# The product of swished z with the returned outputs of mixers A and B: on GpSimd instead of VectorE

## What is computed

```python
merged = None
for i, y_i in enumerate((ya, yb, yc)):
    z = cols(COL_Z + i * BRANCH_WIDTH, BRANCH_WIDTH)
    g = cols(COL_G + i * D_MODEL, D_MODEL)
    u = jax.nn.sigmoid(g) * ((y_i * jax.nn.silu(z)) @ w_br[i])
    merged = u if merged is None else merged + u
out = merged @ w_out
return x + gate[:, None, :] * out
```

## Time and profile before

| | |
|---|---|
| median of 3 runs | 2335.7 us (2334.45 to 2336.24) |
| profiled execution, first to last instruction | 2334.2 us |
| TensorE busy | 2289.5 us |
| VectorE busy | 1669.9 us |
| ScalarE busy | 1123.4 us |
| GpSimd busy | 58.5 us |
| mean granted TensorE clock | 0.999 |

### The profile page before, as it was taken

How to read it: one execution, slowest core, us unless ns; L and a number is a source line. 1 busy time by engine, 2 the same in 40 slices (tenths; PEclk the granted TensorE clock), 3 DMA queues, 4 the chain that set the end, 5 groups by cost and what they waited for, 6 DMA issues and landing times.

```text
span 2334.2 us, 42068 instructions
## 1 busy us (share of the span) xinstructions
PE 2289.5 (98%) x15370; PEld 2135.9 (92%) x15370; DVE 1669.9 (72%) x4593; ACT 1123.4 (48%) x3077; POOL 58.5 (3%) x103
## 2 busy tenths in 40 slices
PE   7999999999999999999999999999999999999999
PEld 5888889999998999999888899899999989999998
DVE  7877677777765766676578867777877667676772
ACT  5666565444444443344356765754444353343440
POOL 0010110000000000000001002100000000000000
PEclk9999999999999999999999999999999999999999
DMA  7221321111113243221521121121110223333223
GB/s 283 95 76 56 122 62 60 58 57 60 56 64 103 74 125 118 93 90 64 173 82 35 35 82 44 58 83 60 56 59 33 82 99 99 102 113 97 88 89 119
DMA packets 74556, 198.72 MB, mean 85 GB/s; under 512 B 10864, under 2 KB 31984, under 8 KB 71408
## 3 DMA queue, kind: packets, MB, share of 16 engines
q1 hardware_dynamic: 59232, 170.29, 21.7%
q10 hardware_dynamic: 15120, 25.74, 3.1%
HBM read 175.02 MB, written 18.87 MB: 83 GB/s over the span
## 4 chain that ended last, share of the span: by engine, by line
PE 81%; DVE 8%; ACT 4%; issue 3%; DMA 3%; SPq 0%; DVEq 0%; ACTq 0%
PE ps_proj L1046 51%; PE ps_score L1092 8%; PE ps_pt L1092 7%; PE ps_pt L1241 2%; PE ps_score L1225 2%; PE ps_pv L1277 2%; PE ps_score L1209 1%; PE ps_pv L1258 1%; PE ps_tr L1292 1%; DMA y_part<-parked 1%; PE ps_tr L1293 1%; PE ps_pv L1271 1%; DVE top L2120 1%; DMA first_ada<-in_w_first 1%; DMA s_raw<-in_w_gate 1%
## 5 line engine op out<-in xcount | busy, mean ns | idle before, releaser
L1046 PE MATMUL ps_proj<-w_hi,act_hi 128*128 128x384 f32 x1824 | 633.7, 347 | 2.2 <-ACT act_hi L1502 1.3
L1046 PE MATMUL ps_proj<-w_hi,act_lo 128*128 128x384 f32 x1824 | 612.7, 336 | 0.0
L1046 PE MATMUL ps_proj<-w_lo,act_hi 128*128 128x384 f32 x1824 | 612.4, 336 | 0.0
L1046 PEld LDWEIGHTS ps_proj<-w_hi,act_hi 128*128 128x128 f32 x1824 | 343.1, 188 | 7.3 <-ACT act_hi L1502 4.8
L1046 PEld LDWEIGHTS ps_proj<-w_lo,act_hi 128*128 128x128 f32 x1824 | 343.8, 188 | 0.0
L1046 PEld LDWEIGHTS ps_proj<-w_hi,act_lo 128*128 128x128 f32 x1824 | 342.9, 188 | 0.0
L2049 DVE TENSOR_REDUCE ssq<-square 128x2 f32<-128x256 f32 (+1 forms) x228 | 95.6, 419 | 207.0 <-ACT square L1600 206.4
L1600 ACT ACTIVATE square<-ps_proj 128x256 f32<-128x256 f32 x228 | 88.1, 387 | 263.8 <-PE ps_proj L1046 263.4
L2426 DVE TENSOR_TENSOR w_lo<-w_raw,w_hi 128x1536 fp32r<-128x1536 f32 (+3 forms) x105 | 169.2, 1612 | 22.3 <-ACT w_hi L1426 21.5
L1426 ACT ACTIVATE w_hi<-w_raw 128x1536 fp32r<-128x1536 f32 (+2 forms) x104 | 144.3, 1388 | 42.5 <-DMA w_raw<-in_w 19.7
L2338 DVE TENSOR_TENSOR s_lo<-s_raw,s_hi 128x512 fp32r<-128x512 f32 x224 | 150.9, 686 | 1.7
(11 more groups left out here) (263 smaller groups left out, 5089.8 us busy)
## 6 DMA issues: line engine op xcount, KB each, us to landing
w_raw<-in_w SPq DMA_DIRECT2D x80, 768.0 KB, 5.7
s_raw<-in_w_gate SPq DMA_DIRECT2D x96, 256.0 KB, 3.2
w_ada<-in_w_mod SPq DMA_DIRECT2D x11, 1536.0 KB, 6.7
w_raw<-in_w SPq DMA_DIRECT2D x24, 512.0 KB, 3.8
wb_raw<-in_w_branch SPq DMA_DIRECT2D x24, 512.0 KB, 3.6
first_ada<-in_w_first SPq DMA_DIRECT2D x8, 1024.0 KB, 12.7
w<-in_w_gate SPq DMA_DIRECT2D x32, 256.0 KB, 3.8
parked<-y_t ACTq DMA_DIRECT2D x4, 1536.0 KB, 5.1
```

Of the source, the lines that this page charges most:

```text
L1046: op = pe.matmul(out, sta[s](k), mov[m](k), start=(k == 0 and n == 0), stop=(k == chunks - 1 and n == 2))
```

## The change

`swish_y` moves from VectorE's program to GpSimd's: the same waits, the same operands, the same semaphore raised. On GpSimd it is called at the same units, ahead of the biases of a unit. Nothing else differs.

```diff
--- before.py
+++ after.py
@@ -1032,8 +1032,16 @@
                             op = pool.tensor_tensor(out.rearrange("p (r k c) -> p r k c", r=4, k=4), win, mp, ALU.add)
                     op.then_inc(*bias_ready.inc((l, h, part)))
 
+            def swish_y(g, block_):
+
+                pool.wait_ge(*y_part_in.at((g, block_)))
+                pool.wait_ge(*swished.at((g, block_)))
+                pool.tensor_tensor(z_sig[block_][:], z_sig[block_][:], y_part[:], ALU.mult).then_inc(*yz_part.inc((g, block_)))
+
             pool.wait_ge(later_in, 16 * 4)
             for n, u in enumerate(UNITS):
+                for g, m in SWISHED_IN.get(n, ()):
+                    swish_y(g, m)
                 if u[0] == "q" and u[5] == 5 and (u[2] == "B" or u[2:4] == ("A", 3)) and u[2:4] != ("B", 3):
                     biases(u[1], (u[3] + 1) % HEADS)
 
@@ -2298,12 +2306,6 @@
                 value = ps_score[:, 0:HALF] if block_ == (0, 0) else sig_of[block_][:]
                 dve.tensor_tensor(z_sig[block_][:], value, z_sig[block_][:], ALU.mult).then_inc(*swished.inc((g, block_)))
 
-            def swish_y(g, block_):
-
-                dve.wait_ge(*y_part_in.at((g, block_)))
-                dve.wait_ge(*swished.at((g, block_)))
-                dve.tensor_tensor(z_sig[block_][:], z_sig[block_][:], y_part[:], ALU.mult).then_inc(*yz_part.inc((g, block_)))
-
             def combine(g, c):
 
                 before = group_before(g)
@@ -2490,8 +2492,6 @@
                             out_low(l, k)
                 if swishes and u2[4] == 4:
                     swish(u2)
-                for g, m in SWISHED_IN.get(n, ()):
-                    swish_y(g, m)
                 for a in TOPPED.get(n, ()):
                     if not first_tops:
                         tops(a)
```

## The result

Against the kernel before on the same chips (20 runs of each), the changed kernel takes 2340.2 us (2336.97 to 2344.7) where the kernel before takes 2336.2: a ratio of 1.002, 95% interval 1.0014 to 1.0026. It is slower by 4.0 us, with 3.3 to 6.1 inside the interval. Five of all the runs reported here took between 2806 and 7890 us, one of these 20 of the kernel before among them (4097.93 us), and are left out of every median. The forecast was 1.4 us faster, its range ended at 2340.0. The time lies just outside the range and on the other side of no change.

A forecast was written before the change was run, and what follows sets the result against it. TensorE, busy 98% of the span, was taken to bound the kernel, so only its waits counted. Gap two's −8.8 and gap one's +7.4 gave −1.4 us, 2335.7 to 2334.3 us, range 2329.8 to 2340.0.

The forecast's parts named there:

- gap two: TensorE's idle before unit T3 in each swished group, from VectorE waiting for y_part; closes, 1.10 us each, −8.8 in all.
- gap one: TensorE's idle before unit T2 in each swished group, ended by W21's load; grows 0.93 us each, +7.4 in all.
- The GpSimd product: The 128x384 float32 multiplication moved to GpSimd, 32 times, taken as 1.13 us each against VectorE's 0.56.
- The turns: GpSimd and VectorE each wait for the other's whole instruction, then finish their own usual time less 0.14 us.
- W21's landing: W21's load, issued behind the second y_part load, is issued and lands 0.93 us later, and T2 starts 0.93 later.
- The other blocks: Blocks two to four on GpSimd: third and fourth y_part loads go some 2 and 1 us earlier, off TensorE's path.
- Rival 2: Fourth block's GpSimd product holds up s_lo of W21, TensorE 0.45 us late per group, +3.6, 2337.9 us; chance 0.13.
- The store's path: First product's store to yz_kept, ahead of ScalarE's sigmoid and s_hi of T2, lands 0.9 us later, hidden by 1.7.
- Rivals 1, 3 and 4: GpSimd quicker, 2330.5, 0.20; GpSimd waiting until VectorE has no two-input work, 2347.7, 0.05; gap two staying, 2343.1, 0.04.
- Around the span: The 1.5 us between the profiled span and the median run time, taken as unchanged.

The follow-up runs named there:

- first_on_vector: Changed kernel with the first block's product back on VectorE, the other three on GpSimd; 2331.6 us, ratio 0.9981 to the kernel before.
- w21_first_gpsimd: Changed kernel with W21's load issued on SyncE ahead of the second block's y_part load; 2331.8 us, ratio 0.9983 to the kernel before.
- changed_look3: Changed kernel with no edit, a further profile; 2344.2 us, span 2342.1.
- both_ends_gpsimd: Changed kernel with W21's load ahead of the second y_part load and ScalarE's s_hi of T2 one unit earlier; 2330.4 us, ratio 0.9979.
- high_early_gpsimd: Changed kernel with only ScalarE's s_hi of T2 one unit earlier, SyncE's order as it was; 2339.3 us, ratio 1.0016 to the kernel before.
- late_load: Kernel before, all products on VectorE, with two idle loads put ahead of W21's load on SyncE; 2350.4 us, ratio 1.0062.
- changed_again: Changed kernel with no edit, run and profiled once more; 2339.3 us, ratio 1.0016 to the kernel before, span 2336.5.
- first_only_gpsimd: Changed kernel with only the first block's product on GpSimd, the other three back on VectorE; 2345.8 us, ratio 1.0039 to the kernel before.
- changed_look2: Changed kernel with no edit, a further profile; 2344.4 us, span 2342.3.
- w21_first_vector: Kernel before, all products on VectorE, with W21's load ahead of the second y_part load on SyncE; 2334.5 us, ratio 0.9993.
- third_later_vector: Kernel before with the third product one unit later on VectorE and its store one unit later on ScalarE; 2334.9 us, ratio 0.9998.
- both_ends_split: both_ends_gpsimd with the first block's product on VectorE and the other three on GpSimd; 2332.4 us, ratio 0.9987 to the kernel before.

## Why the prediction was wrong

**Which way it goes.** Right: TensorE's 16 waits are 8, gap two closes in all eight groups, gap one grows, and it grows through W21. first_on_vector and w21_first_gpsimd each cut one link of that chain, and each turns the loss into a gain.

**The GpSimd product.** Forecast 1.13 us alone; 1.01 to 1.02 measured, 0.12 less. The estimate of 0.84 for 384 columns, worked out from 4497 ns for 2048 (the Trainium skill, GPSIMD Engine Reference, "Elementwise — side-by-side cycle accounting"), is 0.17 too short; the measurement decides.

**The turns.** Right in kind. The first block's product takes 1.33 beside VectorE and 1.01 when VectorE stands still, and VectorE's two s_lo take 1.92 for 1.29. It ends at 814.30; from the start of the swish product that is 2.03 after, 1.21 before: 0.82 later, where 0.93 was forecast.

**Gap one.** Forecast +7.4. The first profile says +7.2, and 14.41 − 5.86 = +8.6 on the mean of four profiles. The product's 0.82 alone would make 6.6; what is above it is W21's landing, which takes 4.47 us on the mean of the eight groups before (4.2 to 4.8), and 4.55, 4.63, 4.68 and 4.97 in the four profiles after (4.1 to 6.2): 0.24 more in each group, 1.9 in all. The step moved W21's landing along with its issue and let it take as long as before. Why it takes longer on the mean, no run isolates.

**Gap two.** Forecast −8.8, measured −7.6 where nothing comes between: 11.57 less 10.62 in each of eight groups. The gap does go, but the term took every unit behind T2 at 2.08, and T4 and the b units still start a little late: the starts of W21, T4 and the b units (827.59, 829.74, 831.92) are 2.15 and 2.18 apart, 0.17 more than twice 2.08. The reading of before was a little high as well: by the prediction's own rule (T2 to b less 10.51) the eight groups are 1.02 to 1.13, 8.5 in all, where it had them at up to 1.17 and took 1.10. On the mean of four profiles it is −7.3, since four of their 32 groups take 0.2 to 0.5 more, by waits at T3, W21 or T4.

**The other blocks.** The third y_part load was forecast earlier by 2 us, as it was (issued at 818.36), but it landed 5.1 us later, not 3. So the third product began at 823.48, beside the s_lo of T3 that closes gap two, which took 0.93 for 0.68. It was hidden. Rival 2 (a meeting at the W21 unit) came in one of 32 groups of the changed kernel (0.35 us, in changed_look3), and in several of first_on_vector and both_ends_gpsimd, where the loads are earlier. Rivals 1, 3 and 4 didn't come. The store's path was hidden, as forecast; high_early_gpsimd bears that out.

**Around the span, and at its end.** Taken as 1.5 and unchanged; it is 1.80 (1.74 to 1.88) in the kernels without GpSimd products in all four blocks and 2.03 in the changed one: +0.24. Inside the span, VectorE's last operation starts 0.74 us after the start of the last matmul in the changed kernel and 0.39 before: +0.4. The sum has neither, and what they are, I don't know.

**The step that failed** is one that isn't there. The sum priced a pause of TensorE as its own length and put the clock behind it at nothing. Gap one went from 1.07 us at most to between 1.13 and 3.29, and behind some of the long ones TensorE ran for 3.4 us at 1.2 GHz, at 1.55 us each. late_load shows it with GpSimd idle, and neither kernel that splits the pause has one behind it. Over four profiles there are 8 spells, 2 to an execution: +3.1 us, against 1.2 missed at gap one and 1.5 at gap two.

These two misses alone turn the sign: +8.6 − 7.3 is +1.3, where −1.4 was forecast. That W21's landing would take as long as before, and that every unit behind T2 would take 2.08, are the two steps that had the direction wrong; the spells are the largest single miss and carry the time out of the range. The whole account on the mean of the four profiles is +8.6 − 7.3 + 3.1 + 0.4 (behind the last matmul) + 0.2 (ahead of and between the groups) = +5.0 on the span, and 5.2 with the 0.2 around it. Two of the four executions are among the slowest of this kernel, so this is more than the +4.0 by the medians. The mean clock of the 29 runs is 0.9982, that of the 96 of the kernel before 0.9993; at 3.4 us of half clock to a spell I estimate from it 1.5 spells more to an execution, +2.3 us, and +4.4 in all. The range missed the time for the same reasons: its upper end was put together from port meetings that hold up the W21 unit, of which one came in 32 groups. That it missed by only 0.2 us is luck: the meetings it was made of are not what made the kernel slow.

**What stays open.** Whether a given pause brings a spell isn't settled. The pauses with a spell behind them were 1.97 to 3.42 us long, and others of 2.00 to 2.30 (in changed_again, changed_look3, first_only_gpsimd and late_load) had none, so the length alone doesn't tell. The spell at 345 us, behind pauses of 1.02 us and less, says the same. Nor is it explained why some executions reach the first swished group 1.5 to 3.6 us late, changed_look2 and first_only_gpsimd among them: most of it is lost in the first 24 us of the program, far ahead of the moved work. In the three latest (first_only_gpsimd 3.6, w21_first_vector 2.6, third_later_vector 2.2) the granted clock stands at 0.50 there for 6.8 to 10.2 us from 21 or 23 us on; changed_look2 is 1.5 late without that. And why both_ends_split has more meetings is open.

## What to carry to other kernels

Before moving a product to GpSimd, follow what its end releases: if a DMA queue waits for it with someone else's load behind, its slower pace is paid in full, and then the order of that queue is the better edit. It took a second one here, since another path stood close behind: on VectorE the order alone gave 0.9993, not clear of no change, and with one copy on ScalarE moved as well it brought 6.2 us, with nothing on GpSimd. Price a pause of a busy TensorE not by its length alone: where an edit makes one grow from 1 us to 2, allow for the clock behind it. Two pauses of some 0.4 to 1.3 us with two units of work between them brought no spell in either profile here, where one of 2 us often did. And an offload that frees VectorE helps only where VectorE's own work isn't slowed by it: with gap one out of the way, the same move gained nothing and cost about 1 us.

## What the runs showed of the hardware

- TensorE's granted clock can fall to 0.50 behind one pause of some 2 us in a kernel that keeps it 98% busy, and need not. It stays there for 3.4 us, with matmuls of 128x384 starting 0.32 apart in place of 0.173. In the 13 such spells behind a gap one, it fell between 0.1 us before TensorE went on and 1.5 us after. It also fell behind three pauses close together, the longest of 1.02 us (at 345 us of the kernel before), in six of 18 profiles.
- GpSimd's 128x384 float32 product takes 1.01 us alone, VectorE's 0.56. Where they meet, both pay: 1.34 for 1.01 on GpSimd, and on VectorE 2.04 for 1.22 (wb_lo) and 1.51 for 0.68 (s_lo). The Trainium skill (SBUF — State Buffer, "Who interferes with whom") has the port pair that both share as an exclusive lock. The trace agrees: the first block's product, which finds VectorE's combination under way, takes 1.34 and not 1.01.
- The same 256 KB load (W21) lands 4.1 to 6.2 us after its issue where a y_part load is issued just ahead of it, in every group and profile of the changed kernel. Issued ahead of that load (w21_first_gpsimd and w21_first_vector) it landed after 3.5 to 4.3. What decides within either range, no run isolates.
